# Output projection of a two-block model: the residual rows added by fp32 matmuls with the identity inside the product's PSUM group, instead of transposes and a VectorE addition

## The reference: what is computed

```python
        mixed = jnp.concatenate([att.astype(x.dtype), ml, cv.astype(x.dtype)], axis=-1)
        x = x + jnp.einsum('bse,ed->bsd', mixed, w_out[l])
    return x
```

## Time and profile before

| what | value |
|---|---|
| median of three runs | 3976.76 us (3969.87 to 3977.34) |
| the profiled execution, its own time | 3972.81 us |
| span of the profiled execution | 3971.0 us |
| mean granted TensorE clock | 0.941 of 2.4 GHz |
| TensorE matmuls busy | 3483.5 us, 88% of the span |
| VectorE busy | 1736.9 us, 44% |
| GpSimd busy | 1346.3 us, 34% |
| ScalarE busy | 899.1 us, 23% |
| last part, 3775 us to the end | 16 steps of the projection |

### The profile page before, as it was taken

The page is one execution under the profiler, slowest core; times in us unless marked ns, Lnnn a source line. Parts: engine busy times, 40 slices in busy tenths (PEclk is TensorE's granted clock), DMA queues, the critical chain, the costliest instruction groups (busy, mean ns, idle before and its releaser), DMA issues. The chain is left out here.

```text
span 3971.0 us, 42813 instructions
## 1 busy us (share of the span) xinstructions
PE 3483.5 (88%) x16444; PEld 2843.4 (72%) x16444; DVE 1736.9 (44%) x1884; ACT 899.1 (23%) x1325; POOL 1346.3 (34%) x863
## 2 busy tenths in 40 slices
PE   2444799999999999999999999999899997975599
PEld 1233587888888777888878888888778885864387
DVE  6965214333332546861133333335368734634521
ACT  2111213111111333111231111112331114534310
POOL 3982024333333524231334333335332223113321
PEclk8677899999999999999999999999999998988799
DMA  6114521111111112233311111111122324038533
GB/s 218 54 38 88 151 68 39 53 48 48 51 50 48 53 48 85 96 117 107 116 48 43 50 51 48 48 48 42 59 80 94 103 80 175 12 79 188 142 111 103
DMA packets 150286, 315.47 MB, mean 79 GB/s; under 512 B 12008, under 2 KB 86760, under 8 KB 147336
## 3 DMA queue, kind: packets, MB, share of 16 engines
q1 hardware_dynamic: 134184, 271.78, 23.0%
q10 hardware_dynamic: 15984, 42.08, 2.8%
HBM read 242.45 MB, written 71.37 MB: 79 GB/s over the span
## 5 line engine op out<-in xcount | busy, mean ns | idle before, releaser
L1285 PE MATMUL ps_job<-AHL,WH 128*128 128x512 f32 x4480 | 1381.2, 389 | 19.2 <-POOL WL L998 17.6
L998 POOL TENSOR_TENSOR WL<-WR,WH 128x1024 fp32r<-128x1024 f32 x216 | 524.2, 2427 | 1511.6 <-ACT WH L783 1511.6
L1285 PEld LDWEIGHTS ps_job<-AHL,WH 128*128 128x128 f32 x4480 | 841.3, 188 | 195.9 <-issue 18.7
L1285 PE MATMUL ps_job<-AHL,WL 128*128 128x512 f32 x2240 | 872.1, 389 | 0.0
L783 ACT CAST WH<-WR 128x1024 fp32r<-128x1024 f32 x216 | 227.5, 1054 | 1632.8 <-PE ps_job L1285 1469.1
L1285 PEld LDWEIGHTS ps_job<-AHL,WL 128*128 128x128 f32 x2240 | 420.8, 188 | 87.7
L1169 DVE TENSOR_TENSOR X<-X,ps_job 128x1024 f32<-128x1024 f32 x128 | 156.1, 1220 | 435.0 <-PE ps_job L1285 354.4
L1285 PE MATMUL ps_job<-FH,WH 128*128 128x512 f32 x768 | 298.8, 389 | 0.0
L1285 PE MATMUL ps_job<-FL,WH 128*128 128x512 f32 x768 | 298.8, 389 | 0.0
L1285 PE MATMUL ps_job<-FH,WL 128*128 128x512 f32 x768 | 298.8, 389 | 0.0
L1159 DVE SCALAR_TENSOR_TENSOR SG<-ps_job,RB 128x1024 f32<-128x1024 f32 x64 | 78.4, 1225 | 446.1 <-PE ps_job L1285 430.3
(11 more groups left out here) (398 smaller groups left out, 5286.9 us busy)
## 6 DMA issues: line engine op xcount, KB each, us to landing
WR<-in_wall SPq DMA_DIRECT2D x248, 512.0 KB, 3.5
fm_scratch<-V ACTq DMA_DIRECT2D x32, 512.0 KB
tm_scratch<-V ACTq DMA_DIRECT2D x28, 512.0 KB
ca_scratch<-s_ca SPq DMA_DIRECT2D x16, 544.0 KB, 2.9
s_ca_out<-ca_scratch SPq DMA_DIRECT2D x8, 1088.0 KB, 8.6
s_xin<-in_x_chunk SPq DMA_DIRECT2D x16, 512.0 KB, 3.8
s_U<-in_x_group SPq DMA_DIRECT2D x2, 4096.0 KB, 18.1
s_mt<-z_scratch SPq DMA_DIRECT2D x64, 128.0 KB, 4.7
```

What stands on the lines that cost most here:

```text
L998: pool.tensor_tensor(dst, raw, src.bitcast(F32), ALU.subtract).then_inc(raw_free, 1)
L1285: last = pe.matmul(out, l, r, start=(k == 0 and i == 0), stop=(k == k_tiles - 1 and i == 2))
```

## The change

The transposes, their PSUM tiles' use and the VectorE copy go. At the end of each half of the product (a PSUM bank of 512 output features) four fp32 matmuls are added to the same accumulation group. Each has a residual tile of x as stationary operand and the 128 x 128 identity as moving operand, and adds 128 columns. TensorE waits for x only in the middle of the step, after the first half's 24 products. VectorE only copies the finished `y_ps` to `y`. SyncE's load of x for tile c now waits for `y_done` of tile c - 2, the last reader of that buffer, instead of `turned`.

```diff
--- before.py
+++ after.py
@@ -2227,7 +2227,7 @@
                 sp.wait_ge(ml_done, c + 1)
                 sp.sem_inc(ready, 1)
                 sp.dma_start(m[:, s], src_m).then_inc(ld_m[s], 16)
-                sp.wait_ge(turned, c + 1)
+                sp.wait_ge(y_done, c + 1)
                 sp.sem_inc(ready, 1)
                 sp.dma_start(x[:, s], src_x).then_inc(ld_x[s], 16)
 
@@ -2348,13 +2348,9 @@
                     dve.tensor_tensor(acc[:, t, at], acc[:, t, at], z[:, t, at], ALU.mult).then_inc(out_done, 1)
 
             def add(c, s):
-                dve.wait_ge(turned, c + 1 + 2)
                 dve.wait_ge(st[s], 8 * c + (16 - 8 * s))
-                ys = y[:, s].rearrange("p (a n) -> p a n", a=2)
-                dve.tensor_copy(ys, x_ps[s][:]).then_inc(xs_copied, 1)
                 dve.wait_ge(y_done, c + 1 + 2)
-                dve.wait_ge(xs_copied, c + 1)
-                dve.tensor_tensor(ys, ys, y_ps[s][:], ALU.add).then_inc(add_done, 1)
+                dve.tensor_copy(y[:, s].rearrange("p (a n) -> p a n", a=2), y_ps[s][:]).then_inc(add_done, 1)
 
             with dve.Fori(0, N_OT // 2) as i:
                 for s in range(2):
@@ -2383,11 +2379,7 @@
             pe.wait_ge(xc_done, C_TILES * N_CN)
 
             def step(c, s, first):
-                pe.wait_ge(ld_x[s], 8 * c + (16 - 8 * s))
                 pe.wait_ge(add_done, c + 1)
-                for k in range(KD):
-                    last = pe.transpose(x_ps[s][:, k // 4, k % 4 * P:(k % 4 + 1) * P], x[:, s, k], ident[:])
-                last.then_inc(turned, 1)
                 if first:
                     pe.wait_ge(wl_done, N_CN)
                     pe.wait_ge(wl2_done, KD - N_CN)
@@ -2396,8 +2388,12 @@
                     cols = slice(n * (D // 2), (n + 1) * (D // 2))
                     for k in range(KD):
                         for i, (l, r) in enumerate(((mh, wh), (ml, wh), (mh, wl))):
-                            last = pe.matmul(y_ps[s][:, n], l[:, s, k], r[:, k, cols], start=(k == 0 and i == 0),
-                                             stop=(k == KD - 1 and i == 2))
+                            pe.matmul(y_ps[s][:, n], l[:, s, k], r[:, k, cols], start=(k == 0 and i == 0), stop=False)
+                    if n == 0:
+                        pe.wait_ge(ld_x[s], 8 * c + (16 - 8 * s))
+                    for k in range(KD // 2):
+                        last = pe.matmul(y_ps[s][:, n, k * P:(k + 1) * P], x[:, s, n * (KD // 2) + k], ident[:], start=False,
+                                         stop=(k == KD // 2 - 1))
                 last.then_inc(y_done, 1)
 
             for s in range(2):
```

## The result

The changed kernel took 3988.23 us (median of 6 runs, 3981.04 to 3994.34), the kernel before 3972.53 us in the six runs now shown for it (3965.71 to 3977.34). The ratio is 1.0034, with a 95% interval of 1.0019 to 1.0049: slower by 0.19% to 0.49%, or 7.5 to 19.5 us with 13.5 in the middle. The difference of the two medians is 15.7 us; the forecast was 15.9.

What follows compares the result with a forecast made beforehand. TensorE alone was taken to bound the projection. 13.8 us in steps 2 to 16, 1.79 in the first and 0.34 for switches made 15.9 us, added to 3976.76: 3992.7 us, 0.40% slower, range 3983 to 3998, chance 0.91.

Steps and rivals of the forecast that it cites:

- The bound: Projection stage: TensorE alone bounds it; a nanosecond added to a step from the second on is a nanosecond of span, 15 times.
- Transposes removed: Projection steps 2 to 16: eight transposes a step leave the path, 0.87 us a step, a gain of 13.05 us.
- Identity matmuls added: Each projection step: eight plain fp32 matmuls, 16 records at 0.112 us, pitch read from the matrix LSTM's key products, 1.79 us.
- Switches: TensorE going to short fp32 matmuls and back: one pair more in steps 2 to 16, two in the first, 0.34 us.
- Wait for x and the moved load: Mid-step wait: x needed 18.1 us after issue, lands after 5.2, at worst 11.2; store and m not issued later; cost nothing.
- step 3: Projection step beginning at 3812.4 us before the change, its m issued at 3791.21 and split done at 3804.5.
- VectorE, nothing: Projection: the hidden 1.217 us copy goes, the 1.222 us addition becomes a same-size copy, on the path once at the end; 0.0 us.
- Clock of the first step: First projection step, after 12 us without TensorE work: 2.93 us lost to the lower clock, taken as unchanged.
- the allowance: First projection step: 2.93 us to either side, in case the moment of the clock's rise moves.
- Sum: Whole kernel: 13.8 + 1.79 + 0.34 = 15.9 us more, median 3992.7 us, 0.40% slower.
- Loads exposed: Rival: weight loads bound the identity matmuls, 0.19 us a record instead of 0.112; 36 us plus switches, 4013 us; chance 0.03.
- Single pass: Rival: each identity matmul is one instruction at the transposes' 0.109 us; 3978.0 us, no measurable change; chance 0.03.

## Why the prediction was right

- **The bound.** Right: TensorE alone in steps 2 to 16, before, after and in every experiment. A removed record was worth its pitch (the run without a residual), an added one too (identity twice), and VectorE's work nothing (copy twice).
- **Transposes removed, 13.05 us.** Measured without them: 15 x 0.89 = 13.4 us. The term was right; the 0.02 us a step more are put down to the switch that goes with them.
- **Identity matmuls added, 16 x 0.112 = 1.79 us a step.** Measured 16 x 0.1117. The row of the key products was the right one to read.
- **Switches, 0.02 us a pair.** Measured 0.013, together with the wait in the middle. With it a step was forecast to grow by 0.94 us and grew by 0.919, which makes 0.3 us over 15 steps.
- **Wait for x and the moved load, nothing.** Right: a delay of one more step did not show. In the changed kernel x's load lands in 4.2 us (median), sooner than the 5.2 before; the store and the load of m that now come behind it land later, 4.3 us against 2.9 and 4.8 against 4.0, and PE waits for neither. (The "step 3" of that part counts tiles from 0; it is the fourth step of the chain.)
- **VectorE, nothing.** Right; the last copy takes 1.22 us like the addition it replaces.
- **Clock of the first step.** This term was off. I took no change in the 2.93 us lost there; the first step grew by 0.93 us and not by the 1.83 of its matmuls and switches, since less was lost to the lower clock, 2.1 us (7.52 - 5.46) instead of 2.93. The step took 14.8 us where near 15.7 was forecast. The loss moves from one execution to the next: the first 24 products take 7.52 us in the changed kernel and 8.28 in the run with x loaded later, and the first 48 take 13.83 us in the kernel before and 12.97 in the one with VectorE's copy twice, with the same TensorE program each time. It was within the allowance, and nothing shows that the change had a part in it.
- **Sum.** 14.7 us in the profiled executions from the first product on, 15.7 on the medians, 15.9 forecast. That the last two agree within 0.2 us is luck: the runs of one kernel lie up to 13 us apart, and the ratio's interval spans 7.5 to 19.5 us. What the traces bear out is the growth of a step, 15 times. The absolute time, 3992.7, came out 4.5 us too high because the median of three that it started from was 4.2 us above the median of six.
- **Loads exposed.** The rival's time was not seen, but my argument against it was wrong in part. I said that next to nothing of the weight loads is on the path. They do run beside the matmuls, and yet they set the pitch: with half the columns the step did not get shorter. What was wrong in the rival was its 0.19 us, the length of a load and not the distance between two.
- **Single pass.** The rival's premise fell, its price was right: one record for each tile gives 11.78 to 11.80 us a step, both as a transpose and as an fp32r matmul.

## What to carry to other kernels

On a stretch that TensorE bounds, price each added matmul by its records and their pitch in a like stream: with 128 fresh weight columns a record cost 0.11 us here, whether it moved 128 columns or 64. A plain fp32 identity matmul is two such records and a transpose one, so a residual went into the PSUM group more cheaply as a transpose that opened it. Before moving work between engines, look for the engine that waits: here VectorE had 149 us idle, and letting it turn the residual gave 13 us where relieving it cost 16. Compare profiled executions from a common point on when what lies ahead moves by more than the change.

## What the runs showed that I had not expected

- Half the columns made the short matmuls no cheaper, and the step even 0.07 us (fp32) and 0.03 us (one pass) longer: the products behind them took 5.54 us instead of 5.46 in the chain. Why was not tried.
- A transposing fp32 matmul can open a group to which fp32r products of 512 columns then add, at the pitch of an ordinary transpose.
- Loading the residual in pieces of 128 bytes, four times as many, did not slow a stream of 14 tiles: the four transfers of a tile land in 4.7 us each (median), against 5.2 for the one of before. The DMA share rose to 0.67 for it, so a stage with busier transfers might pay; that was not tried.
